# Queries and keys split at projection eviction, projection and attention in one section, the first head loaded under the last three blocks

## What is computed

```
h = rmsnorm(x, rms_g) * (1 + scale) + shift
q, k, v, z_a, glu, z_b, gates = split(h @ w_in + b_in)      # 5632 columns
y_a = attend(q, k, v) * silu(z_a)
y_b = conv_branch(glu) * silu(z_b)                          # 31 taps, layernorm, silu
m = g_a * (y_a @ w_proj_a) + g_b * (y_b @ w_proj_b)         # g = sigmoid(gates)
y = rmsnorm(x + gate * (m @ w_out), final_g)
```

## Time and profile before

| | us |
|---|---|
| median of three runs | 2085.68 |
| profiled execution | 2082.15 |
| its span, first to last instruction | 2080.4 |
| TensorE busy | 1926.1 |
| VectorE busy | 1117.2 |
| ScalarE busy | 489.1 |
| GpSimd busy | 296.6 |

### The profile page before, as it was taken

How to read it: one execution, slowest core, us unless ns; L and a number is a source line. 1 busy time by engine, 2 the same in 40 slices (tenths; PEclk the granted TensorE clock), 3 DMA queues, 4 the chain that set the end, 5 groups by cost and what they waited for, 6 DMA issues and landing times. The chain is left out here.

```text
span 2080.4 us, 31012 instructions
## 1 busy us (share of the span) xinstructions
PE 1926.1 (93%) x11491; PEld 1692.8 (81%) x11491; DVE 1117.2 (54%) x1878; ACT 489.1 (24%) x982; POOL 296.6 (14%) x350
## 2 busy tenths in 40 slices
PE   7999999999999999999999558999996899959998
PEld 1788899888888888888888458898896799957886
DVE  2543221168408831881387078877875666645443
ACT  1541100111101111111111035555553211101011
POOL 0000000000000000000000146454440222212321
PEclk9999999999999999999999769999998899989999
DMA  7623221112202221222011553554621765535432
GB/s 236 203 71 130 84 74 59 46 62 83 77 21 71 86 76 29 79 74 68 31 69 54 118 106 71 131 103 111 111 68 68 249 201 200 165 119 186 170 121 101
DMA packets 205679, 217.56 MB, mean 105 GB/s; under 512 B 49804, under 2 KB 176636, under 8 KB 202364
## 3 DMA queue, kind: packets, MB, share of 16 engines
q1 hardware_dynamic: 190120, 196.06, 31.5%
q10 hardware_dynamic: 15443, 19.97, 2.7%
HBM read 143.60 MB, written 72.39 MB: 104 GB/s over the span
## 5 line engine op out<-in xcount | busy, mean ns | idle before, releaser
L685 PE MATMUL ps_ring<-h_hi,w_hi 128*128 128x512 f32 (+1 forms) x1600 | 592.9, 371 | 6.3 <-DVE w_lo L489 4.5
L686 PE MATMUL ps_ring<-h_lo,w_hi 128*128 128x512 f32 (+1 forms) x1600 | 589.4, 368 | 0.0
L687 PE MATMUL ps_ring<-h_hi,w_lo 128*128 128x512 f32 (+1 forms) x1600 | 589.3, 368 | 0.0
L625 DVE SCALAR_TENSOR_TENSOR conv_acc<-glu_out,taps,conv_acc 128x773 f32<-128x773 f32 x360 | 369.1, 1025 | 12.2
L685 PEld LDWEIGHTS ps_ring<-h_hi,w_hi 128*128 128x128 f32 x1600 | 302.0, 189 | 59.2 <-DVE w_lo L489 4.9
L687 PEld LDWEIGHTS ps_ring<-h_hi,w_lo 128*128 128x128 f32 x1600 | 301.8, 189 | 50.7
L686 PEld LDWEIGHTS ps_ring<-h_lo,w_hi 128*128 128x128 f32 x1600 | 302.1, 189 | 49.4
L430 ACT ACTIVATE out_stage<-ps_ring,param_cols 128x512 f32<-128x512 f32 (+1 forms) x140 | 90.7, 648 | 576.7 <-PE ps_ring L687 576.7
L1399 PE MATMUL ps_proj<-y_hi,wp_hi 128*128 128x256 f32 x576 | 165.3, 287 | 1.6 <-POOL y_lo L1355 1.6
L1400 PE MATMUL ps_proj<-y_lo,wp_hi 128*128 128x256 f32 x576 | 163.8, 284 | 0.0
L1401 PE MATMUL ps_proj<-y_hi,wp_lo 128*128 128x256 f32 x576 | 163.7, 284 | 0.0
(11 more groups left out here) (150 smaller groups left out, 2814.2 us busy)
## 6 DMA issues: line engine op xcount, KB each, us to landing
proj<-out_stage SPq DMA_DIRECT2D x128, 256.0 KB, 2.0
w_raw<-in_w_in SPq DMA_DIRECT2D x44, 512.0 KB, 3.9
gates_in<-proj SPq DMA_DIRECT2D x9, 2048.0 KB, 11.4
q_raw<-proj SPq DMA_DIRECT2D x16, 576.0 KB, 7.8
k_raw<-proj SPq DMA_DIRECT2D x16, 576.0 KB, 9.4
merged<-m_out ACTq DMA_DIRECT2D x9, 1024.0 KB, 10.8
m_in<-merged SPq DMA_DIRECT2D x9, 1024.0 KB, 5.3
w_ada<-in_w_ada SPq DMA_DIRECT2D x8, 1024.0 KB, 12.4
```

Of the source, the lines that this page charges most:

```text
L625: op = dve.scalar_tensor_tensor(dst, src, tap, dst, ALU.mult, ALU.add)
L685: pe.matmul(out, w_hi[:, s, k], h_hi[c][:, k], start=first, stop=False)
L686: pe.matmul(out, w_hi[:, s, k], h_lo[c][:, k], start=False, stop=False)
L687: op = pe.matmul(out, w_lo[:, s, k], h_hi[c][:, k], start=False, stop=last)
```

## The change

Three things are changed together.

1. The queries and keys are split when a projection unit is evicted. The factor 1/8 of the queries, now with a minus sign, is put into their weights. ScalarE writes the high part (for queries in the order of the tiles), VectorE subtracts it from the PSUM bank and writes the low part, both are stored to DRAM tensors of their own, `q_hi`, `q_lo`, `k_hi`, `k_lo`. Two small units follow each key block, `sk` (turns the keys of the context for their output) and `ck` (turns the cached keys, which are split in the same way). The order of the blocks is new.
2. The front section and attention share one block of instructions. The last three blocks of the projection run chunk by chunk. When their third chunk is done, SyncE loads head 0 into the memory of the first three chunks of `h`, and GpSimd makes its tables. Attention is written out without a loop, and without the extra instruction of `wait_reg` after its waits.
3. A tile's window scores and context scores stand side by side in two neighbouring banks, and `soften` goes over both with a table that is zero over the context. It takes a minimum, as the scores are negative; one exp with scale -1 covers the tile. ScalarE copies the last window block of the turned probabilities with the context's.

The core of the diff (the attention section is indented anew as a whole and is cut here):

```diff
-    single = g + z
-    out = q + k[:3] + v[:2] + k[3:] + v[2:]
+    single = z + g[4:]
+    out = g[:3] + q + v[:2] + k[:1] + v[2:] + k[1:] + g[3:4]
     for i in range(4):
-        out += list(glu[i]) + single[6 * i:6 * i + 6]
+        out += list(glu[i]) + single[5 * i:5 * i + 5]
...
-    while n < len(blocks):
+    while n < len(blocks) - 3:
...
+    return units + [(blocks[m][0], m, c) for c in range(5) for m in range(n, n + 3)]
...
+    early_done = spot(nb - 1, 2)
...
+                if kind in split_kinds:
...
+                    sp.dma_start(hi[row:row + P, at:at + w], ohi[:, s, 0:w].bitcast(F32)).then_inc(out_d[s], 16)
+                    sp.dma_start(lo[row:row + P, at:at + w], olo[:, l, 0:w].bitcast(F32)).then_inc(low_d[l], 16)
...
+            if u == early_done:
+                load_first(sp)
...
             load_ada(0)
             load_ada(1)
-            load_ada(2)
             load_x(0)
+            load_ada(2)
+            load_w(sp, 0)
             load_ada(3)
-            load_w(sp, 0)
...
+                dve.wait_ge(ev_act, on_act[u])
+                src, hi, lo = ps[:, u % 4, 0:w], ohi[:, s, 0:w].bitcast(F32), olo[:, l, 0:w]
...
+                elif kind == "q" and c < 4:
+                    for b in range(4):
+                        op = dve.scalar_tensor_tensor(grouped(lo)[:, b], tile_order(src)[:, b], bias_of(kind, col),
+                                                      grouped(hi)[:, b], ALU.add, ALU.subtract)
+                else:
+                    op = dve.scalar_tensor_tensor(lo, src, bias_of(kind, col), hi, ALU.add, ALU.subtract)
...
+        def load_qk(n):
+            if n >= 2:
+                sp.wait_ge(s_mm, TPH * (n - 1))
+            u, rows = n % 2, slice(DH * n, DH * n + DH)
+            for half in range(2):
+                part = slice(DH * half, DH * half + DH)
+                sp.dma_start(q_sp[u][part].bitcast(F32), (io.q_hi, io.q_lo)[half][rows]).then_inc(qk_in[u], 16)
+                sp.dma_start(k_hi[u][part].bitcast(F32), io.k_hi[rows]).then_inc(qk_in[u], 16)
+                sp.dma_start(k_lo[u][part].bitcast(F32), io.k_lo[rows]).then_inc(qk_in[u], 16)
...
+        def load_first(q):
+            q.wait_ge(io.unit_mm, io.early_units)
+            io.qkv_stored(q)
+            load_qk(0)
+            load_window(q, 0)
...
+            load_v(0)
...
+        for n in range(2, HEADS):
+            load_qk(n)
+            load_window(sp, n)
+            load_v(n)
+            if n % 2:
+                store_y(n // 2 - 1)
+                load_z(n // 2)
...
+            if m == 0:
+                pe.wait_ge(io.ev_act, io.all_act)
+                pe.wait_ge(io.ev_dve, io.all_dve)
...
+                dve.tensor_tensor_reduce(s_sb[:, m % 2, 0:nk + CTX], ps_s[m % 2][:, 512 - nk:768],
+                                         tables[n % 2][:, off:off + nk + CTX], 1.0, 3e38, ALU.add, ALU.min,
+                                         stat[:, m % 4, 0:1]).then_inc(red, 1)
...
+            act.activation(p_sb[:, m % 2, 0:nk + CTX], src, ACT.Exp, bias=stat[:, m % 4, 0:1], scale=-1.0).then_inc(exp_done, 1)
...
+            if nb:
+                act.activation(pT[0:w4, m % 2, nb - 1], ps_t[1][0:w4, 2], ACT.Copy)
+            act.activation(pT[:, m % 2, 4:6], ps_t[1][:, 0:2], ACT.Copy).then_inc(pt_act, 1)
...
+        pool.wait_ge(io.unit_mm, io.early_units)
+        fill(0)
+        bias_tables(0)
```

More of the change, by code:

```diff
@@ L141, in modulation @@
         if kind != "v" or c % 2 == 1:
-            stores[u] = slot_of[u]
+            stores.add(u)
             per_slot[slot_of[u]] += 32 if kind == "v" and c == 17 else 16
+        if kind in split_kinds:
+            low_of[u], low_free[u] = lo_n % 3, low_per_slot[lo_n % 3]
+            low_per_slot[lo_n % 3] += 16
+            lo_n += 1
+        if kind in ("q", "k", "ck", "v"):
+            qkv_out = list(per_slot)
+    full_of = {n: slot_of[u] for u, (kind, n, c) in enumerate(units) if kind == "k" and c == 4}
     done_after = {}
@@ new lines, in modulation @@
+    acc, acc_at = put("conv_acc", [P, 2, 776])
+    vbias, _ = put("v_bias", [P, WA])
+    square = nc.alloc_sbuf_tensor_at("square", [P, D], BF16, offset=mem + u_at + 16384)
+    rows, _ = put("param_rows", [P, P], at=out_at)
+    c_rows, _ = put("cond_rows", [2 * KC, P], at=out_at + 512)
+    taps, _ = put("tap_rows", [P, P], at=out_at + 1536)
+    x_at = {0: hi_at[3], 1: lo_at[3], 2: hi_at[3], 4: lo_at[3], 3: u_at}
+    xs = {c: put(f"x_rows{c}", [P, CHUNKS[c][1] // P, D], at=x_at[c])[0] for c in PREP}
@@ new lines, in front_stored, with qkv_stored, front_pool @@
+    def front_stored(sp):
+        for s in range(3):
+            sp.wait_ge(out_d[s], per_slot[s])
+        for s in range(2):
+            sp.wait_ge(conv_d[s], 32 * 6)
+        sp.wait_ge(grow_out, 64)
+    def qkv_stored(sp):
+        for s in range(3):
+            sp.wait_ge(out_d[s], qkv_out[s])
+            sp.wait_ge(low_d[s], low_per_slot[s])
+        sp.wait_ge(tab_out, 16 * QC)
+    def front_pool(pool):
+        pool.memset(half[:], -0.5).then_inc(half_set, 1)
+        pool.wait_ge(half_set, 1)
+        tiles = 0
+        for j, c in enumerate(PREP):
+            w = CHUNKS[c][1] // P
+            tiles += w
+            t = slice(4 * c, 4 * c + w)
+            pool.wait_ge(sq_done, tiles)
+            if j:
+                pool.wait_ge(rms_done, 2 * j)
+            pool.tensor_scalar(tmp[:, 0:w], ssum[:, t], 1.0 / D, EPS, ALU.mult, ALU.add).then_inc(rms_done, 1)
+            pool.wait_ge(rms_done, 2 * j + 1)
+            pool.tensor_tensor(rstd[:, t], tmp[:, 0:w], half[:, 0:w], ALU.pow).then_inc(rms_done, 1)
@@ L750 @@
 ST = (QR - 1) * BW_C + BW_R * BW_C
-MASKED = -1e30
+MASKED = 1e30
 LT = 16
 TPH = LT + CTX // P
-TPP = 2 * TPH
-RED = 2 * LT + CTX // P
 NG = 3
+NT = HEADS * TPH
 KW = TOK + CTX
@@ new lines, in attend @@
+    head_buffers(0)
+    window, win_c = put("bias_window", [P, BW_R * BW_C]), put("bias_cols", [P, 3, 512])
+    rmask, cmask = put("row_mask", [P, 3, 16]), put("col_mask", [P, 3, 32])
+    assert used[0] <= 3 * 2 * KC * 512 * 4
+    s_sb, p_sb, pT = put("scores", [P, 2, 768]), put("probs", [P, 2, 768]), put("probs_t", [P, 2, 6, P])
+    stat = put("stat", [P, 4, 2])
+    o_sb, inv = put("o_pair", [P, TPH, 2, DH + 1]), put("inv_sums", [P, NG, 2])
+    o_norm = put("o_normed", [P, 2, NG, P])
+    z_sb, y_sb = put("z_pair", [P, TOK]), put("y_pair", [P, TOK])
@@ L1248 @@
+    io.stack.close()
 CH = 256
```

1754 lines of the change are left out of this document (850 added, 904 removed).

## The result

The changed kernel takes **1997.07 us** (median; 1995.68 to 2000.81) against 2086.33 for the kernel before (2083.55 to 2086.99): ratio 0.9577, 95% interval 0.9561 to 0.9594. The profiled execution took 1995.68 us with a span of 1993.9 (before: 2082.15 and 2080.4).

The account below looks back on a forecast made before the run. TensorE, busy 93% of the span, was taken as the bound, with a hole at the border and idle time in attention. Border -37.8 and attention -26.5 gave -64.3: profiled 2082.15 to 2017.9, median 2021 us, range 2006 to 2048.

Parts of the forecast that it names:

- The start: First loads: reordered, but the same bytes ahead of the third weight block; 0 us, bounds -3 and +3.
- The projection: Front section: VectorE's subtractions in the eviction path cost 0, bounds 0 and +10 us; front ends at 1171.9.
- rival B: Projection: TensorE waits for VectorE's subtractions, or key transpositions wait for copies; +25 us, 2046; chance 0.07.
- The border: Between projection and attention: early loads of head 0 bring first turned probabilities to 1184.2 from 1222.0, -37.8 us.
- Rival C: Border loads: queries and keys come at 340 GB/s; 2011, or 2003 with no wait in attention; chance 0.08.
- Attention: First turn to last `ya` store: less idle time, half clock and key transpositions; 377.9 to 351.4 us, -26.5.
- Idle time: Attention: 29.7 us of TensorE's idle time, laid to splitting, goes; 7.8 and 3.4 us come back.
- The sizes of the new operations: Attention: `soften` 0.72 to 0.95 us, single exp 0.75 to 0.94; ScalarE's loop 2.1 us against a 2.35 us slot.
- Rival A: Attention: idle time is the turn between three engines and stays, with ScalarE's longer order; 2043; chance 0.19.
- Rival D: Attention: each head's loads on SyncE's queue come too late and starve it; 2095 at 100 GB/s; chance 0.03.
- Rival E: Border: a wait ahead of head 0's loads is late and the hole stays; +38 us, 2059; chance 0.03.
- Merge and output: Behind attention: untouched by the change, 0 us.

Follow-up runs that it names:

- stacked runs: Changed kernel with two score rows per tile and an unused splitting load: 0.9662 (2015.71 us); with one gate per tile as before too: 0.9714 (2027.34 us).
- a_rows: Changed kernel with two score rows per tile again, context minimum taken separately and two exps, splitting still in the projection: 0.9604 (2001.85 us).
- a_late: Changed kernel with head 0's loads and tables behind the last projection unit, not under the last three blocks: 0.9704 (2023.07 us).

## Why the prediction was wrong, step by step

**The start, first failed step.** "The first loads are reordered, but the same bytes stand ahead of the third weight block, on which the third unit waits: 0, bounds -3 and +3." That is right for the loads (1.0007), but it was the whole of what I priced there. The third weight block isn't held by bytes but by a buffer, and the buffer by VectorE's queue, where the change moves `low(0)` ahead of three splits. Size: 8.5 us, outside both bounds. I had followed SyncE's queue, and not those of the two engines.

**The projection.** VectorE in the eviction path costs no time that the traces show: TensorE is busy 500.00 of 500 us from 150 to 650 in both traces, and rival B falls. The front end was forecast at 1171.9 and is at 1163.4, exactly the 8.5 us of the start lower.

**The border** came out as said, partly by luck. First turned probabilities 36.4 us behind the first load, 36.3 forecast; hole 11.8 for 10.6; TensorE's two scores without a gap. Inside, three errors cancel: the window lands after 25.1 us and not 22.2, the tables take 9.8 us and not 10.8, and from there to the first turn it is 1.6 and not 3.3, because the table load of the exp (1172.09) lies under the tables. For 4.26 MB the landing means 170 GB/s, or 184 behind the 2 us that the prediction set apart. The chip moved 200 GB/s in that time, near the 211 of the earlier trace rows; what I had left out are the stores and value loads that share it. Rival C (340 GB/s) falls. The Trainium skill, "DMA: Bandwidth & Descriptors", section Bandwidth, gives the 341 GB/s weighed in the prediction, measured there on loads of 1 MB issued from GpSimd. For these loads of SyncE's the measurement decides: the ten-microsecond stretches from 1140 to 1170 have 219, 204 and 182 GB/s. The same trace moves 347 to 350 GB/s in the merge (1520 to 1550), so that it is the border's loads that are slow, and why they are was not tried.

**Attention, second failed step.** "377.9, less 29.7 idle (...), less 6.7 (...), less 3.8 (32 transpositions) = 337.7. Back come 2.3% idle as in the last head, 7.8; 3.4 for the chain of the last group, unchanged; and 2.5" for the clock: 351.4. Measured are 334.5, 16.9 less and below even the floor of 337.7. Three terms were mis-sized.

- *Idle time.* 7.8 and 3.4 should have come back, 11.2. TensorE is idle 3.8 us in attention (busy 330.65 of 334.46): 7.4 of the 16.9.
- *Clock.* The sum holds 5.3 us of loss by half clock behind the first turn. Half clock lasts 5.0 us there (to 1181.4) and costs half of that, 2.5. That is 2.8 less.
- *Work.* The rest, 6.7. I took busy time for work. In 84 us at full clock in both traces, the kernel before is busy 77.59 us for 649 records, 11.96 us per hundred, the changed one 83.63 for 722, 11.58 (first row before, second after). In the trace of the kernel before a product of 512 columns is recorded with 0.39 us, and the next starts after 0.23 (1159.70 and 1159.93), so a short wait between two can show as busy.

```profile
1302.00:1386.00 84.00, 77.59 (x649) 74.75 (x648) 66.63 (x195) 47.55 (x133) 40.90 (x58) 1.00 0.57 125
```

```profile
1302.00:1386.00 84.00, 83.63 (x722) 82.43 (x721) 52.64 (x133) 50.08 (x145) 19.79 (x24) 1.00 0.75 159
```

The mechanism behind the idle term was wrong too. I gave all idle time to the splitting, but for what the last head keeps. By the stacked runs splitting was right only together with the second softening pass (18.4 us), and two edits that I had priced at nothing are worth 12.2 us (the gates' order) and 8.9 (the loops and the extra instruction behind each wait). The last head's share was no floor either: between 1542 and 1590 its named waits are 0.8 us for ScalarE's copies and 0.2 for the gates. The changed kernel has no wait of TensorE's for ScalarE between 1225 and 1495, and `a_rows`, with its second exp, brings back 3.1 us of such waits.

**The sizes of the new operations** held: `soften` 724 to 958 ns for 544 to 768 columns (0.72 to 0.95 forecast), the single exp 741 to 928 ns (0.75 to 0.94), ScalarE's longer order no bound. Rival A falls: behind 1180 TensorE has one wait above 0.2 us in attention, 1.6, for the last group. Rival D falls: no head waits for its tables. Rival E falls: the loads start at 1140.0. `a_late` gives its price as 26 us where I had 38; it keeps the queries and keys split, which E's price did not.

**Merge and output**, forecast 0, are +2.5, which is within what this stretch varies by in kernels that don't change it (480.5 to 483.9).

## What to carry to other kernels

When a diff moves an operation in an engine's queue, follow the semaphore it raises: a load into a double buffer waits for the last reader of the buffer, and an operation of 1.2 us that stands 7 us too late held the whole start. To ask what an engine's work costs, stack the loads: each alone cost 3 to 5 us of attention, with VectorE 71 to 74% busy, and both together 18, at 82%. And when a wait is taken away and another wait for the same engine grows, look at that engine's whole queue, not at the wait.

## What the runs showed of the hardware

SyncE's issue of a load isn't always half a microsecond: with the DMA engines busy throughout, five loads took it 12.62 us, and the stores behind them came late by that. TensorE's busy time at full clock held about 3% of slack in a stretch with many short waits (11.96 us per hundred records for 11.58), which only the count of records showed. An idle time that ends in "issue" can be a real wait for another engine: 3.79 us of it were a wait for a memset of GpSimd. The same section of the same kernel differs between executions: 377.9 to 381.3 us for attention and 480.5 to 483.9 for merge and output, so that a difference of 3 us from one trace is no finding.
